# Query head norms of a two-block transformer kernel: one accumulating sum on four column groups, instead of 32 separate ones

## What is computed

```
q = apply_rope_2(rmsnorm(q.reshape(B, T, 16, 64), q_g), cos, sin)
k = apply_rope_2(rmsnorm(k.reshape(B, T,  4, 64), k_g), cos, sin)
```

## Time and profile before

| what | value |
|---|---|
| median of 3 runs | 2562.28 us |
| the profiled execution's own time | 2562.14 us |
| its span in the profile | 2560.6 us |
| PE busy | 2525.1 us (99%) |
| DVE, POOL, ACT busy | 52%, 49%, 39% |
| mean granted TensorE clock | 0.998 |

### The profile page before, as it was taken

How to read it: one execution, slowest core, us unless ns; L and a number is a source line. 1 busy time by engine, 2 the same in 40 slices (tenths; PEclk the granted TensorE clock), 3 DMA queues, 4 the chain that set the end, 5 groups by cost and what they waited for, 6 DMA issues and landing times.

```text
span 2560.6 us, 34168 instructions
## 1 busy us (share of the span) xinstructions
PE 2525.1 (99%) x13842; PEld 2075.8 (81%) x13842; DVE 1339.1 (52%) x2305; ACT 986.9 (39%) x1685; POOL 1243.5 (49%) x609
## 2 busy tenths in 40 slices
PE   8999999999999999999999999999999999999999
PEld 5668888888777888888877888888888888888887
DVE  4884999943225699983875522124245223532121
ACT  4475423223357432233476433223233223432231
POOL 5875444444456454443686344443444344444442
PEclk9999999999999999999999999999999999999999
DMA  4111655632320455642401333223322222333321
GB/s 144 56 34 52 204 197 181 210 103 71 108 70 18 138 193 196 197 148 84 143 22 34 99 99 95 91 98 121 127 87 83 93 88 82 99 99 99 99 95 70
DMA packets 261040, 277.12 MB, mean 108 GB/s; under 512 B 7316, under 2 KB 249620, under 8 KB 260628
## 3 DMA queue, kind: packets, MB, share of 16 engines
q1 hardware_dynamic: 259284, 272.32, 32.8%
q10 hardware_dynamic: 1600, 2.62, 0.3%
HBM read 270.21 MB, written 2.10 MB: 106 GB/s over the span
## 4 chain that ended last, share of the span: by engine, by line
PE 95%; DVE 2%; ACT 1%; POOL 1%; issue 0%; DMA 0%; SPq 0%; ACTq 0%; DVEq 0%
PE bank L532 24%; PE bank L534 24%; PE bank L533 24%; PE bank L667 3%; PE bank L712 2%; PE bank L626 2%; PE bank L628 2%; PE bank L627 2%; PE bank L695 2%; PE bank L551 1%; PE bank L491 1%; PE bank L934 1%; PE bank L552 1%; PE bank L553 1%; PE bank L482 1%; PE bank L483 1%
## 5 line engine op out<-in xcount | busy, mean ns | idle before, releaser
L1904 POOL TENSOR_TENSOR wlo<-raw,whi 128x1024 fp32r<-128x1024 f32 (+1 forms) x408 | 995.8, 2461 | 1203.3 <-ACT whi L990 1110.3
L990 ACT ACTIVATE whi<-raw 128x1024 fp32r<-128x1024 f32 (+1 forms) x408 | 405.6, 1041 | 564.3 <-PE bank L534 488.8
L532 PE MATMUL bank<-Xhi,whi 128*128 128x512 f32 (+1 forms) x1568 | 617.2, 394 | 0.0
L533 PE MATMUL bank<-Xlo,whi 128*128 128x512 f32 (+1 forms) x1568 | 610.5, 389 | 0.0
L534 PE MATMUL bank<-Xhi,wlo 128*128 128x512 f32 (+1 forms) x1568 | 610.4, 389 | 0.0
L532 PE MATMUL bank<-Hhi,whi 128*128 128x512 f32 x976 | 379.9, 389 | 0.0
L534 PE MATMUL bank<-Hhi,wlo 128*128 128x512 f32 x976 | 379.7, 389 | 0.0
L533 PE MATMUL bank<-Hlo,whi 128*128 128x512 f32 x976 | 379.7, 389 | 0.0
L532 PEld LDWEIGHTS bank<-Xhi,whi 128*128 128x128 f32 (+1 forms) x1568 | 293.3, 187 | 68.5 <-issue 6.6
L534 PEld LDWEIGHTS bank<-Xhi,wlo 128*128 128x128 f32 (+1 forms) x1568 | 293.2, 187 | 63.1
L533 PEld LDWEIGHTS bank<-Xlo,whi 128*128 128x128 f32 (+1 forms) x1568 | 293.4, 187 | 62.3 <-issue 1.7
(11 more groups left out here) (303 smaller groups left out, 3371.7 us busy)
## 6 DMA issues: line engine op xcount, KB each, us to landing
ada<-in_ada_w SPq DMA_DIRECT2D x48, 1024.0 KB, 5.1
raw<-in_w_up SPq DMA_DIRECT2D x32, 1024.0 KB, 5.6
raw<-in_w_down SPq DMA_DIRECT2D x32, 1024.0 KB, 5.0
raw<-in_mlp_w_in SPq DMA_DIRECT2D x32, 1024.0 KB, 5.3
raw<-in_mlp_w_out SPq DMA_DIRECT2D x32, 1024.0 KB, 5.0
raw<-in_gmlp_w_in SPq DMA_DIRECT2D x24, 1024.0 KB, 5.0
raw<-in_gmlp_w_out SPq DMA_DIRECT2D x12, 1024.0 KB, 5.1
raw<-in_w_in_a SPq DMA_DIRECT2D x8, 1024.0 KB, 5.2
```

Source lines behind the costliest of these rows:

```text
L532: pe.matmul(b[0:rows, :], whi[s][:, c, j:j + rows], hi[:, c, :], start=(c == 0), stop=False)
L533: pe.matmul(b[0:rows, :], whi[s][:, c, j:j + rows], lo[:, c, :], start=False, stop=False)
L990: act.activation(whi[u % 2][:, c0:c1, 0:k], src[:, c0:c1, 0:k], ACT_F.Copy).then_inc(hi_done, 1)
L1904: pool.tensor_tensor(wlo[u % 2][:, c0:c1, 0:k], src[:, c0:c1, 0:k], whi[u % 2][:, c0:c1, 0:k].bitcast(F32), ALU.subtract).then_inc(lo_done, 1)
```

## The change

The squares become the moving operand. The stationary operand is a window of 32 columns of a new constant `head_sel` (128 x 62, zero but for columns 30 and 31, which hold 1/64 for one head each). For chunk c the window begins at 30-2c, so that the two heads land in rows 2c and 2c+1 of 32 rows. The four token blocks go to the four groups of 32 partitions of bank 6, and all eight chunks accumulate there. ACT takes one root of the 128x128 result into `QS`, now before it copies `vc` tile 1 and not tile 2; PE turns `QS` into the next 128 columns of bank 6 after `vc` tile 1; DVE reads its reciprocal from there. PE begins the scores when that reciprocal is set, where it waited for ACT's root. `head_sel` is loaded by SP behind `rope_b`, on the same semaphore.

```diff
         def query_means(c):
             pe_until.wait_ge(held_in, 18 + c)
             if c == 0:
                 pe_until.wait_ge(hn_root, 1)
+                pe_until.wait_ge(rope_in, 48)
             for i in range(NT):
-                m = pe.matmul(bank[6][:, 16 * i + 2 * c:16 * i + 2 * c + 2], tmp[c % 2][:, i * P:(i + 1) * P], head_mean[:, 0:P:64], start=True, stop=True)
+                m = pe.matmul(bank[6][32 * i:32 * i + 32, 0:P], head_sel[:, 30 - 2 * c:62 - 2 * c], tmp[c % 2][:, i * P:(i + 1) * P], start=(c == 0), stop=(c == KC - 1))
             m.then_inc(qn_sum, 1)
...
         def after_vc(o):
             if o == 0:
                 query_means(7)
+            if o == 1:
+                pe_until.wait_ge(qn_root, 1)
+                pe.transpose(bank[6][:, P:2 * P], QS[:], ident[:]).then_inc(qn_turn, 1)
             if o == 2:
                 pe_until.wait_ge(rot_sum, 17)
                 pe_until.wait_ge(key_copy, 8)
-                pe_until.wait_ge(qn_root, 1)
+                pe_until.wait_ge(qn_set, 1)
                 steps_c(0, 2)
...
         def evac_vc(o):
-            if o == 2:
+            if o == 1:
                 act_until.wait_ge(qn_sum, KC)
-                act.activation(RQ[:], bank[6][:, 0:NT * 16], ACT_F.Sqrt, bias=eps[:, 0:1]).then_inc(qn_root, 1)
+                act.activation(QS[:], bank[6][:, 0:P], ACT_F.Sqrt, bias=eps[:, 0:1]).then_inc(qn_root, 1)
...
-        dve_until.wait_ge(qn_root, 1)
-        dve.reciprocal(RQ[:], RQ[:]).then_inc(qn_set, 1)
+        dve_until.wait_ge(qn_turn, 1)
+        dve.reciprocal(RQ[:].rearrange("p (i h) -> p i h", i=NT), bank[6][:, P:2 * P].rearrange("p (i h) -> p i h", i=NT)[:, :, 0:16]).then_inc(qn_set, 1)
...
                 sp.dma_start(rope_b[:], consts["rope_b"]).then_inc(rope_in, 16)
+                sp.dma_start(head_sel[:], consts["head_sel"]).then_inc(rope_in, 16)
```

More of the change, by code:

```diff
@@ L236, in body @@
         KS = [sb(f"KS{i}", [P, S], F32, region) for i in range(2)]
-        RQ = sb("RQ", [P, NT * 16], F32, region)
+        RQ, QS = sb("RQ", [P, NT * 16], F32, region), sb("QS", [P, P], F32, region)
+        head_sel = sb("head_sel", [P, 62], F32, region)
     with ExitStack() as region:
@@ L285, in body @@
     up_q, h_hi, up_r, h_lo = (sem(n) for n in ("up_q", "h_hi", "up_r", "h_lo"))
-    hn_full, hn_root, hn_rec, hn_out, qn_sum, qn_root, qn_set = (
-        sem(n) for n in ("hn_full", "hn_root", "hn_rec", "hn_out", "qn_sum", "qn_root", "qn_set"))
+    hn_full, hn_root, hn_rec, hn_out, qn_sum, qn_root, qn_turn, qn_set = (
+        sem(n) for n in ("hn_full", "hn_root", "hn_rec", "hn_out", "qn_sum", "qn_root", "qn_turn", "qn_set"))
     z_root, z_recip, z_rows = (sem(n) for n in ("z_root", "z_recip", "z_rows"))
@@ L1492, in rotation_sin @@
                 dve_until.wait_ge(landing, whole)
-            dve_until.wait_ge(rope_in, 16 if r < 15 else 32)
+            dve_until.wait_ge(rope_in, 16 if r < 15 else 48)
             if r >= 2:
@@ L1939, in rotation @@
                 pool_until.wait_ge(landing, whole)
-            pool_until.wait_ge(rope_in, 16 if r < 15 else 32)
+            pool_until.wait_ge(rope_in, 16 if r < 15 else 48)
             pool.tensor_tensor(rotated(r)[0:rows, :], rotated(r)[0:rows, :], rope[0:rows, 0, :], ALU.mult).then_inc(rot_cos, 1)
@@ L2119, in shape_constants @@
         "ident": np.eye(P, dtype=f), "head_mean": np.kron(np.eye(2), np.full((64, 64), 1 / 64)).astype(f),
-        "perm_half": perm_half, "pick": pick, "fold": np.tile(np.eye(32, dtype=f), (4, 1)),
+        "perm_half": perm_half, "pick": pick, "head_sel": np.kron(np.eye(2), np.full((64, 1), 1 / 64)).astype(f) @ np.eye(62, dtype=f)[30:32],
+        "fold": np.tile(np.eye(32, dtype=f), (4, 1)),
         "rope_a": rope_a.astype(f), "rope_b": rope_b.astype(f), "tri": tri, "tsum": tsum,
```

## The result

The changed kernel takes 2565.51 us (median of 21 runs, 2563.00 to 2567.36), the kernel before 2561.64 us (21 runs on the same chips): a ratio of 1.0014 with an interval of 1.0008 to 1.002. That is 3.9 us slower, less than the 0.2% at which the prediction drew its line, and 2.3 us above the top of its range; the forecast was 2561.1 us, a gain of 1.0. The profiled execution took 2565.17 us (span 2563.7), 3.0 more than the one before. It shows the highest mean granted clock of the 21, 0.998; the other 20 show 0.996 or 0.997. What follows explains this one execution, and why most others lost more to the clock stays open.

The account below looks back on a forecast made before the run. PE was taken as the bound (95% of the span), except for a chain over ACT, POOL and DVE before the first scores. 1.5 us gained less 0.5 for the new wait gave 2561.1 us from 2562.14; range 2559.6 to 2563.2.

Parts of the forecast that it names:

- The sums (0.60 us a chunk): PE's sums per chunk: cost 0.60 us (0.58 to 0.66) where they cost 0.91, saving 0.31 each.
- the fourfold speedup: PE's sums by the skill page's up to 4x for 32 columns: 0.26 us a chunk, saving 0.65; not adopted.
- the 2560.7: Total time at the favourable end of the sum's bounds, 1.4 us off; also given for the 0.26 us chunk.
- DVE's floor: ACT's copy of tile 7 cannot start before DVE's sum for tile 4, at 1277.91 if nothing moves DVE.
- Tile 7's copy 1.3 to 1.9 us earlier: ACT's copy after query tile 7: six chunks' saving arrives there as 1.3 to 1.9 us, taken as 1.5.
- From that copy to the last rotary sum nothing changes: Chain from tile 7's copy through swap, POOL's 5.20 us split and rotation to DVE's 0.70: unchanged.
- The new wait, +0.5: PE waits for DVE's reciprocal before the first scores: 0.5 us later (0.46 to 0.7), counted in full.
- Chunks 6 and 7, the turning, the root, the new load at nothing: Between tile 7 and the scores, 0.6 us saving and 0.13 us turning only change idle time; root and load cost nothing.
- Rival A: Before the scores, PE idle grows to 1.9 us; 3.4 us at half clock follow, losing 1.7: 2562.8 us; chance 0.25.
- Rival C: The later half-clock stretch from 1302.8 goes away, gaining at most 1.3 us: 2559.8 us; chance 0.12.
- Rival B: In PE's sums the four groups do not stream together: 1.43 us a chunk, total 2565.9 us; chance 0.05.

Follow-up runs that it names:

- e12_before_nudge: Kernel before, sums untouched, plus two unread 128-zero writes on DVE ahead of query tile 3's sine; median 2561.95 us, ratio 0.9997 to 1.0015.
- e11_pace_more: Changed kernel plus two unread matmuls (512 and 384 columns) on PE ahead of each chunk's sums; median 2562.92 us, ratio 1.0 to 1.0018.
- e9_reordered: Changed kernel with POOL's vc split, one SP weight load and POOL's later split held behind waits, tile 7's rotation first; median 2558.29 us.
- e10_before_reordered: Kernel before, old sums, with POOL's vc split, one SP load and POOL's later split held behind waits, tile 7's rotation first; median 2561.23 us.
- e7_before_rotate_first: Kernel before with POOL's rotation of query tile 7 ahead of the split for the output product's first unit; median 2559.67 us, ratio 0.9987 to 1.0005.
- e1_pace: Changed kernel plus two unread matmuls (512 and 256 columns) on PE ahead of each chunk's sums; median 2566.33 us, ratio 1.001 to 1.0028.
- e5_split_later: Changed kernel with POOL's split for vc held until DVE has summed query tile 3; median 2563.20 us, ratio 1.0001 to 1.0018.

## Why the prediction was wrong

**The sums (0.60 us a chunk): right.** 0.57 measured, 0.01 under the 0.58 to 0.66. The row of L809 decided rightly against the 0.26 us a chunk by the fourfold speedup. What that 0.26 would have made of the time was not worked out to the end: six times 0.65 are 3.9 us at tile 7, not the 1.9 behind the 2560.7, and only DVE's floor could have held them back.

**Tile 7's copy 1.3 to 1.9 us earlier: right in number,** 1.66, and of no use. The floor was the right thing to fear: PE came 2.1 us earlier, and DVE's sum of tile 4, at 1277.44 and not 1277.91, let 1.66 of it through.

**"From that copy to the last rotary sum nothing changes": this step failed.** It took for granted that the chain still begins at tile 7's copy. It begins at tile 6's, whose copy hangs on DVE's sum of tile 3, whose sine stood 0.04 us ahead of POOL's split. I had written that DVE's long entries stand beside POOL's splits and that these move with PE, and took from it a bound on the gain only, with tile 4's sum as the floor. I did not ask what a split that comes earlier does to the DVE work that it now overtakes. Nor did I place SP's load against ACT's swaps, though the chain of queues ran through both. The last rotary sum, forecast 1.5 us earlier, came 0.98 later: 2.5 of the 4.1 us between the forecast gain of 1.0 and the profile's loss of 3.1. The other 1.6 are the clock, which the sum left out (2.75 lost, 1.19 back). The e12_before_nudge run shows that this order alone makes the late chain; e11_pace_more that the change without it lags 0.64 us through the stage.

The Trainium skill's page SBUF — State Buffer (Who interferes with whom) bears on the 0.04 us: it says that a DVE instruction with two SBUF inputs contends with a GpSimd instruction that reads SBUF, and "Issue order, not op shape, decides who blocks." The trace agrees: sine ahead by 0.04 us, 0.68; behind by 0.10 us, 2.85.

**The new wait, +0.5: right.** 0.56, and 0.55 alone in the kernel before.

**Chunks 6 and 7, the turning, the root, the new load at nothing: right** as far as the runs show. They stand nowhere on the account's path, and e9_reordered gains on e10_before_reordered what eight chunks save, which leaves no room for a dear turning.

**Rival A was the right mechanism with the wrong size and cause.** The idle time came to 4.78 us, not 1.9, since the chain was later and not earlier; the lower clock held for the first 5.9 us of scores and `vc`, not 3.4, and cost 2.75, not 1.7. Its chance was taken from rows of one execution, which tell that an answer occurs and not how often: the idle stretch at 753.4, in code that no run changes, was followed by 0.50 in 3 of the 14 profiles (the kernel before, e7_before_rotate_first, e11_pace_more) and by 1.00 in 11. **Rival C** came as well and gave 1.19 back, near its 1.3; I had treated the two as exclusive. **Rival B** did not happen.

## What to carry to other kernels

When a faster step moves a second engine's work earlier, list what that work now overtakes on every engine that it shares a resource with, and look for pairs of starts that lie within a tenth of a microsecond: there the order is luck, and a saving can cost more than it brings. Read not the last producer of a chain alone but the one ahead of it in each in-order queue. Here the saving was had in full once the interfering work was held behind explicit waits.

## What the hardware showed unexpectedly

- Between DVE and POOL it is a matter of turns. POOL's half split takes 2.40 us, the sine 0.68; the sine that comes second ended 0.54 us after the half split that was ahead of it (e1_pace: 2.41 us from 1269.90, sine done at 1272.85), and the sum behind it ended 0.54 us after the second half. Losing one turn cost about 2.2 us: tile 3's sum ended at 1275.64 there, at 1273.40 in the kernel before. DVE's entries with an operand from a PSUM bank kept 0.73 to 0.75 us beside the split.
- A swap issued while a 1 MB load was running moved nothing until the load was nearly done. In the kernel before, the swap's first packet came 1.1 us after its issue (1274.72, 1275.86). In the changed kernel that would be 1277.4, but in the DMA view from 1276.3 to 1278.4 all packets are of the load's queue:

```profile
DMA packets 719, 0.74 MB, mean 351 GB/s; under 512 B 0, under 2 KB 719, under 8 KB 719
...
q1 hardware_dynamic: 719, 0.74, 105.3%
```

  The Trainium skill's page DMA: Bandwidth & Descriptors (Queues, rings and completion order) has each DMA engine take turns between the queues that it has work for, a packet at a time. The trace agrees only from 1278.5 on: up to 1279.3 it has 127 packets of the swap's queue and 107 of the load's. Why no turn came in the microsecond ahead of that is not shown.
- What the clock did after an idle stretch does not follow from the stretch's length alone. The later idle stretch is 2.58 or 2.59 us long in all 14 profiles; 9 show a granted clock of 0.50 after it and 5 show 1.00. Before the scores, idle stretches up to 2.72 us (e1_pace) were followed by 1.00, those from 3.08 us up (e5_split_later) by 0.50. For e1_pace and then e5_split_later, the idle stretch and what followed:

```profile
1289.50:1292.10 2.60, 0.09 (x1) 0.00 (x0) 1.41 (x4) 1.67 (x2) 1.29 (x1) 1.00 0.69 204
1292.20:1295.60 3.40, 3.40 (x21) 2.23 (x22) 2.25 (x8) 1.44 (x5) 0.00 (x0) 1.00 0.40 142
...
1287.80:1290.80 3.00, 0.12 (x2) 0.00 (x1) 1.24 (x3) 1.67 (x2) 1.69 (x2) 1.00 0.40 128
1291.40:1294.80 3.40, 3.40 (x11) 1.45 (x8) 2.15 (x7) 1.52 (x4) 0.00 (x0) 0.50 0.36 129
```

  Nor does it follow from the kernel: the idle stretch of 1.67 us at 753.4 went both ways, as said above, in code that all 14 share. What decides between the two outcomes stays open.
